# First unit of a two-block transformer kernel: norm weights sent in the tokens' rows, another order of loads, low parts moved between VectorE and GpSimd, idle products on TensorE, high products ahead of low ones

## The chip, the cores and the metric

One core of a Trainium2 chip. The metric is the device time of one execution in microseconds, the median over several runs. Below, a profile of one execution stands beside it; its times count from the first instruction.

## The reference

The reference runs two blocks over 512 tokens of width 1024 in float32. The first block puts 16 meta tokens ahead of them (528 in all), and does attention of two kinds, gates and a feed-forward part; the second block is larger. Only the very first step matters here:

```python
h = jnp.concatenate([meta, x], axis=1)
xn = rms_norm(h, norm_gains[layer, 0])          # h * rsqrt(mean(h*h) + EPS) * gain
proj = xn @ w_in[layer]
q_a, k_a, v_a, f_a, q_b, k_b, v_b, g_a, g_b = jnp.split(proj, SPLIT_POINTS, axis=-1)
```

The root of the mean square is one number per token, so the kernel multiplies it in after the product: it computes (h * gain) @ w_in first and scales the result.

## The kernel before, in words

**Units.** All weights stream through as units of 1 MB, 128 x 2048 float32, which is 16 tiles of 128x128: for each of the eight slices k of the width two tiles, c = 0 and c = 1 (a chunk is one c over all k). Two buffers each of `raw`, `whi` and `wlo` alternate between even and odd units. SP loads a unit into `raw` when `lo_done` says that the one before in that buffer has been used (L670 to L675).

**Three products for one.** To keep float32 accuracy with the faster matmul type, each weight is split in a high part (`whi`, ScalarE's cast) and a low part (`wlo` = raw - whi, GpSimd's subtraction, L692), each activation likewise in `xhi` (ScalarE, L844) and `xlo` (VectorE, L1554). TensorE then forms whi * xhi, whi * xlo and wlo * xhi (`tile_products`, L2339 to L2346, the products are on L2344), each over the tokens in two pieces of 256 and 272 columns.

**The start.** Tokens come transposed as `h`, 128 rows by 8 slices k by 528 tokens. SP issues the gains `cv`, four pairs of slices of `h`, and unit 1. ScalarE issues unit 0 in four quarters of 512 columns (a quarter holds the tiles of two k), then `fw0`, `ident` and `masks` (L831 to L836), and then goes through four rounds: cast one quarter of unit 0, make `xhi` of two k (L838 to L845). GpSimd makes the low part of each quarter behind the cast (L695 to L701), VectorE `xlo` of each k behind `xhi` (L1551 to L1556). TensorE takes k by k, with both chunks and all three products (L2432 to L2443). ScalarE then casts unit 1 whole (`hi_of(1)`, L846), loads a table, forms eight squares of `h` (L849) and some small constants; VectorE adds the squares up in seven sums (L1557 to L1561).

**What follows.** TensorE does chunk 0 of unit 1 (`chunk(1, 0, 2)`), then a product of a block of ones with the sum of the squares (L2449), which gives ScalarE and VectorE the total from which they form the roots (L862 to L865 and L1566 to L1574). Meanwhile TensorE runs the 8-column product for the forget gate (L2457) and chunk 1 of unit 1, and then needs the roots (L2463). Units 2, 3 and so on follow with the same counts of signals: `hi_first` and `lo_first` count quarters of the units that are handed on in quarters, `hi_done` and `lo_done` whole units. The lists `QUARTERED` and `HI_FIRST` (L579, L581) say which units those are, and their place in the list is their base in the count.

Every engine works through its instructions in the order of the text; waits are written by hand on named signals.

## Time and profile before

| | |
|---|---|
| median of 3 runs | 2179.92 us (2179.61 to 2180.91) |
| the profiled execution, its own time | 2180.31 us |
| its span, first to last instruction | 2178.5 us |
| instructions | 31351 |
| TensorE busy | 2148.5 us (99%), 12494 products |
| VectorE busy | 994.9 us (46%) |
| ScalarE busy | 754.2 us (35%) |
| GpSimd busy | 1007.5 us (46%) |
| mean granted clock of TensorE | 0.996 |
| data moved | 194.94 MB, mean 89 GB/s |

PE is TensorE's matmul, PEld its loading of weights, DVE VectorE, ACT ScalarE, POOL GpSimd, SP SyncE; an engine with a q behind it is its sequencer, which issues DMAs. The ends of matmuls are modelled, and consecutive ones overlap, so the distance from one start to the next says more than the duration. The granted clock is a share of full speed.

### The profile page before, as it was taken

Reading aid. Unit: us, or ns where it says so; the run is one execution under the profiler, and the core shown is the slowest. Engines: PE = TensorE matmul, PEld = TensorE weight load, DVE = VectorE, ACT = ScalarE, POOL = GpSimd, SP = SyncE. Lnnn points to the kernel's source line nnn. Section 1 sums busy time; section 2 is a strip of 40 time slices with the busy share of each in tenths; the row PEclk is TensorE's granted clock in tenths of the full one; section 3 lists DMA queues with packets and bytes.
Section 4 is the critical chain, followed back from the end, with each engine's and each line's share of the span. In section 5 each row is a group of like instructions: output and inputs, shape, how many; then the busy total and the mean of one; then the engine's idle time right before and its main releaser. Section 6 shows DMA issues by size and latency. Waiting matters only on the chain.

```text
span 2178.5 us, 31351 instructions
## 1 busy us (share of the span) xinstructions
PE 2148.5 (99%) x12494; PEld 1852.2 (85%) x12494; DVE 994.9 (46%) x1458; ACT 754.2 (35%) x1015; POOL 1007.5 (46%) x825
## 2 busy tenths in 40 slices
PE   8999999999999999999999999999999999999998
PEld 7897999999999887888888778878788888888886
DVE  5144454379888207322200819671876442222027
ACT  4133455243222215322212415551336332222134
POOL 4322223455555547555544545254331555555444
PEclk9999999999999999999999999999999999999999
DMA  4321111212222223322222221114220222222222
GB/s 164 102 69 68 59 48 70 97 59 97 96 85 88 106 96 107 125 96 96 97 97 96 91 107 42 59 59 151 81 78 21 97 97 97 96 96 97 96 100 93
DMA packets 31838, 194.94 MB, mean 89 GB/s; under 512 B 3968, under 2 KB 4480, under 8 KB 9984
## 3 DMA queue, kind: packets, MB, share of 16 engines
q1 hardware_dynamic: 26352, 182.66, 23.5%
q10 hardware_dynamic: 5392, 10.95, 1.6%
q8 instruction: 68, 1.11, 0.2%
q14 instruction: 26, 0.21, 0.0%
HBM read 189.24 MB, written 4.23 MB: 89 GB/s over the span
## 4 chain that ended last, share of the span: by engine, by line
PE 84%; issue 7%; DVE 4%; POOL 3%; ACT 1%; DMA 0%; SPq 0%; DVEq 0%; POOLq 0%; ACTq 0%
PE ps L2344 74%; POOL wlo L692 3%; PE ps L2939 2%; DVE sqa L1500 1%; PE ps L3152 1%; PE ps L3136 1%; PE ps L3072 1%; PE ps L3019 1%; DVE x2lo L1488 1%; PE ps L2623 1%; PE ps L2646 0%; PE ps L3117 0%; PE ps L2682 0%; PE ps L3162 0%; DMA h<-h 0%
## 5 line engine op out<-in xcount | busy, mean ns | idle before, releaser
L692 POOL TENSOR_TENSOR wlo<-raw,whi 128x512 fp32r<-128x512 f32 (+2 forms) x820 | 1006.1, 1259 | 1145.3 <-ACT whi L758 1041.4
L758 ACT CAST whi<-raw 128x2048 fp32r<-128x2048 f32 x162 | 309.6, 1911 | 815.1 <-PE ps L2344 757.2
L2344 PE MATMUL ps<-x2hi,whi 128*128 128x512 f32 x1136 | 449.1, 395 | 1.2 <-DVE x2lo L1488 1.1
L2344 PE MATMUL ps<-x2hi,wlo 128*128 128x512 f32 x1136 | 442.8, 390 | 0.0
L2344 PE MATMUL ps<-x2lo,whi 128*128 128x512 f32 x1136 | 442.5, 390 | 0.0
L2344 PE MATMUL ps<-xhi,whi 128*128 128x256 f32 (+2 forms) x1336 | 273.0, 286 | 11.9 <-DVE xlo L1554 9.5
L2344 PE MATMUL ps<-xlo,whi 128*128 128x256 f32 (+2 forms) x1336 | 270.6, 284 | 0.0
L2344 PE MATMUL ps<-xhi,wlo 128*128 128x256 f32 (+2 forms) x1336 | 270.4, 284 | 0.0
L2344 PEld LDWEIGHTS ps<-x2hi,whi 128*128 128x128 f32 x1136 | 213.4, 188 | 49.9 <-issue 5.6
L2344 PEld LDWEIGHTS ps<-x2lo,whi 128*128 128x128 f32 x1136 | 213.5, 188 | 44.6 <-issue 1.7
L2344 PEld LDWEIGHTS ps<-x2hi,wlo 128*128 128x128 f32 x1136 | 213.3, 188 | 44.7
L2344 PEld LDWEIGHTS ps<-xhi,whi 128*128 128x128 f32 x1336 | 208.2, 191 | 13.1 <-POOL wlo L692 12.2
L2344 PEld LDWEIGHTS ps<-xhi,wlo 128*128 128x128 f32 x1336 | 208.3, 191 | 0.0
L2344 PEld LDWEIGHTS ps<-xlo,whi 128*128 128x128 f32 x1336 | 208.3, 191 | 0.0
L2344 PE MATMUL ps<-hlo,whi 128*128 (+1 forms) x528 | 205.6, 389 | 0.0
L2344 PE MATMUL ps<-hhi,whi 128*128 (+1 forms) x528 | 205.6, 389 | 0.0
L2344 PE MATMUL ps<-hhi,wlo 128*128 (+1 forms) x528 | 205.6, 389 | 0.0
L2344 PEld LDWEIGHTS ps<-hhi,whi 128*128 128x128 f32 x528 | 99.2, 188 | 20.6
L2344 PEld LDWEIGHTS ps<-hlo,whi 128*128 128x128 f32 x528 | 99.2, 188 | 20.6
L2344 PEld LDWEIGHTS ps<-hhi,wlo 128*128 128x128 f32 x528 | 99.2, 188 | 20.3
L1512 DVE TENSOR_TENSOR cvl<-ps,fold 128x1024 f32<-128x1024 f32 x22 | 26.9, 1224 | 189.3 <-PE ps L2344 189.3
L1985 DVE SCALAR_TENSOR_TENSOR h<-ps,h 128x512 f32<-128x512 f32 x16 | 10.9, 682 | 209.7 <-PE ps L2344 209.7
(467 smaller groups left out, 2763.0 us busy)
## 6 DMA issues: line engine op xcount, KB each, us to landing
raw<-wstream SPq DMA_DIRECT2D x170, 1024.0 KB, 4.8
h<-h SPq DMA_DIRECT2D x4, 528.0 KB, 8.4
ncb<-c_rows ACTq DMA_DIRECT2D x8, 256.0 KB, 3.5
ple_rows<-ple_out ACTq DMA_DIRECT2D x4, 512.0 KB, 4.3
bias<-bias_rows ACTq DMA_DIRECT2D x8, 256.0 KB, 4.8
ple<-ple_rows ACTq DMA_DIRECT2D x4, 512.0 KB, 5.7
out_dram<-outb SPq DMA_DIRECT2D x8, 256.0 KB, 2.9
raw<-wstream ACTq DMA_DIRECT2D x4, 256.0 KB, 7.1
```

The source lines that it names most:

```text
L692: return nc.gpsimd.tensor_tensor(wlo[b][:, cols], raw[b][:, cols], whi[b][:, cols].bitcast(F32), ALU.subtract)
L758: nc.scalar.copy(whi[b][:], raw[b][:]).then_inc(sig("hi_done"), 1)
L1488: vec.scalar_tensor_tensor(out=xl[:, k, 0:T], in0=view(k), scalar=cv[:, gain + k:gain + k + 1], in1=xh[:, k, 0:T].bitcast(F32), op0=ALU.mu ...
L1500: vec.tensor_tensor(squared[:, 0, :], squared[:, 0, :], squared[:, k, :], ALU.add).then_inc(sig("sq_added"), 1)
L1512: return vec.tensor_tensor(dst, pair(src), scale, ALU.mult)
L2344: ins = mm(dst, w[slot][:, cols], xx(tok), start=first and p_ == 0, stop=last and p_ == 2, skip_group_check=True)
L2623: mm(zs[x][:, col + b * P:col + (b + 1) * P], qkb[rows_of(x), 4 + c, b * P:(b + 1) * P], qkb[rows_of(x), c, i * P:(i + 1) * P], start=(q = ...
L2939: ins = mm(gv_bank(half, j), xx[:, k if first else k + 4, tok], ww[u % 2][:, cols], start=(first and k == 0 and p_ == 0), stop=(not first ...
L3019: ins = mm(bank(5 + e)[:, t_ * P:(t_ + 1) * P], gvt[:, s_, (2 * hd + e) * P:(2 * hd + e + 1) * P], rhs, start=(x_ == 0), stop=(x_ == len(p ...
L3072: ins = mm(dst, left, right, start=True, stop=True)
L3136: mm(dst, dq[:, hd, j * P:(j + 1) * P], ckvf[:, 0:w], start=True, stop=False)
L3152: ins = mm(bank(6 + m % 2)[:, 0:P], ckvt[:, b, :], dpt[m % 2][:, b * P:(b + 1) * P], start=(b == 0), stop=(b == j))
```

## The change

1. The gains of the first norm are put in front of the tokens in the same rows: the tensor `hg` is 8 + 8 x 528 columns wide, `h` is a view of it, and `xhi` and `xlo` of the first unit take their scale from `hg`.
2. SP loads `hg` in three pieces: the gains with k = 0; k = 1 and 2; k = 3 to 7. Unit 1 follows, then `fw0`, `ident` and `masks`, which share one signal. ScalarE's queue issues quarter 0 of unit 0, its other three quarters as one DMA, and `cv`.
3. ScalarE's table load stands ahead of its first wait. Unit 1 is cast in quarters and joins the lists of units handed on in quarters.
4. VectorE makes the low parts of unit 0, one quarter ahead of each second `xlo`. GpSimd waits for these to be done and makes those of unit 1, quarter by quarter.
5. VectorE first fills a block of 128x256 with zeros (`idle`). TensorE forms ten float32 products of that block with itself into bank 7, which nobody reads, then waits for the first cast and forms one more.
6. In unit 0 TensorE forms the four high products (whi * xhi, two chunks by two pieces of tokens) of k ahead of the eight others of k - 1. In unit 1 it waits for the low parts by quarters.

```diff
@@ -160,7 +160,8 @@
     tokens = np.concatenate([v["meta_tokens"], v["x"][0]])
-    h0 = np.ascontiguousarray(tokens.T.reshape(KC, P, T1).transpose(1, 0, 2))
+    h0 = tokens.T.reshape(KC, P, T1).transpose(1, 0, 2).reshape(P, KC * T1)
+    h0 = np.concatenate([columns(v["norm_gains"][0][0]), h0], axis=1)
     units += std_units(np.concatenate([v["w_o_fox"][0], v["w_o_sb"][0]]), run_of(0, 8))
@@ -221,7 +222,8 @@
         wlo = [at(f"wlo{b}", [P, UT * P], F32R) for b in range(2)]
-        h = at("h", [P, KC, T1])
+        hg = at("hg", [P, KC + KC * T1])
+        h = hg[:, KC:].rearrange("p (k t) -> p k t", t=T1)
         x_at = place["at"]
@@ -244,6 +246,7 @@
         madds = masks_r[:, P:2 * P]
+        idle = at("idle", [P, HALF], offset=arena)
         ntri_r = at("ntri_r", [P, P], F32R, offset=temp + 14720)
@@ -576,9 +579,9 @@
         PIECE = {u: P for u in (U_UP, U_UP + 1, U_PLEP, U_F1I, U_F1I + 1, U_GR + 2, U_GR + 3, U_MG1, U_DSAO + 1)}
-        QUARTERED = [0, U_UP + 1, U_UP + 2, U_PLEP, U_F1I, U_F1I + 1, U_F1I + 2, U_PLEG + 3]
+        QUARTERED = [0, 1, U_UP + 1, U_UP + 2, U_PLEP, U_F1I, U_F1I + 1, U_F1I + 2, U_PLEG + 3]
         PIECE[U_F1I + 2] = PIECE[U_UP + 2] = BANK
-        HI_FIRST = [0, U_UP + 1, U_UP + 2, U_F1I + 1]
+        HI_FIRST = [0, 1, U_UP + 1, U_UP + 2, U_F1I + 1]
         PIECE[U_PLEG + 3] = P
@@ -663,10 +666,13 @@
         def _(sp):
-            sp.dma_start(cv[:], cvec).then_inc(sig("gains_in"), 16)
-            for q in range(4):
-                sp.dma_start(h[:, 2 * q:2 * q + 2, :], h0[:, 2 * q:2 * q + 2, :]).then_inc(sig(f"h_in{q}"), 16)
+            sp.dma_start(hg[:, 0:KC + T1], h0[:, 0:KC + T1]).then_inc(sig("h_in"), 16)
+            sp.dma_start(hg[:, KC + T1:KC + 3 * T1], h0[:, KC + T1:KC + 3 * T1]).then_inc(sig("part_in2"), 16)
+            sp.dma_start(hg[:, KC + 3 * T1:], h0[:, KC + 3 * T1:]).then_inc(sig("part_in3"), 16)
             sp.dma_start(raw[1][:], wstream[1]).then_inc(sig("raw_ready1"), 16)
+            sp.dma_start(fw0[:], fw).then_inc(sig("consts_in"), 16)
+            sp.dma_start(ident[:], ident_c).then_inc(sig("consts_in"), 16)
+            sp.dma_start(masks[:], masks_c).then_inc(sig("consts_in"), 16)
             with sp.Fori(1, n_units // 2) as i:
@@ -692,17 +698,14 @@
+            pool.wait_ge(sig("lo_done"), 1)
             for q in range(4):
                 if q < 3:
-                    pool.wait_ge(sig("hi_first"), q + 1)
-                    low_part(0, q).then_inc(sig("lo_first"), 1)
+                    pool.wait_ge(sig("hi_first"), 3 + q + 1)
+                    low_part(1, q).then_inc(sig("lo_first"), 1)
                 else:
-                    pool.wait_ge(sig("hi_done"), 1)
-                    low_part(0, q).then_inc(sig("lo_done"), 1)
-            pool.wait_ge(sig("hi_done"), 2)
-            for q in range(3):
-                low_part(1, q)
-            low_part(1, 3).then_inc(sig("lo_done"), 1)
+                    pool.wait_ge(sig("hi_done"), 2)
+                    low_part(1, q).then_inc(sig("lo_done"), 1)
             def low_parts(u, w):
@@ -828,31 +831,31 @@
+            act.dma_start(raw[0][:, 0:BANK], wstream[0][:, 0:BANK]).then_inc(sig("part_in0"), 16)
+            act.dma_start(raw[0][:, BANK:], wstream[0][:, BANK:]).then_inc(sig("part_in1"), 16)
+            act.dma_start(cv[:], cvec).then_inc(sig("gains_in"), 16)
+            nc.scalar.preload_act_table_set("natural_log_exp_and_others")
             for q in range(4):
-                act.dma_start(raw[0][:, q * BANK:(q + 1) * BANK], wstream[0][:, q * BANK:(q + 1) * BANK]
-                              ).then_inc(sig(f"part_in{q}"), 16)
-            act.dma_start(fw0[:], fw).then_inc(sig("fw_in"), 16)
-            act.dma_start(ident[:], ident_c).then_inc(sig("ident_in"), 16)
-            act.dma_start(masks[:], masks_c).then_inc(sig("masks_in"), 16)
-            act.wait_ge(sig("gains_in"), 16)
-            for q in range(4):
-                act.wait_ge(sig(f"part_in{q}"), 16)
+                if q < 2:
+                    act.wait_ge(sig(f"part_in{q}"), 16)
                 cols = slice(q * BANK, (q + 1) * BANK)
                 nc.scalar.copy(whi[0][:, cols], raw[0][:, cols]).then_inc(sig("hi_first" if q < 3 else "hi_done"), 1)
-                act.wait_ge(sig(f"h_in{q}"), 16)
                 for k in (2 * q, 2 * q + 1):
-                    nc.scalar.activation(xhi[:, k, :], h[:, k, :], ACT.Copy, scale=cv[:, G_PRE + k:G_PRE + k + 1]
+                    if k in (0, 1, 3):
+                        act.wait_ge(sig({0: "h_in", 1: "part_in2", 3: "part_in3"}[k]), 16)
+                    nc.scalar.activation(xhi[:, k, :], h[:, k, :], ACT.Copy, scale=hg[:, k:k + 1]
                                          ).then_inc(sig("xhi_ready"), 1)
-            hi_of(1)
-            nc.scalar.preload_act_table_set("natural_log_exp_and_others")
+            act.wait_ge(sig("raw_ready1"), 16)
+            for q in range(4):
+                cols = slice(q * BANK, (q + 1) * BANK)
+                nc.scalar.copy(whi[1][:, cols], raw[1][:, cols]).then_inc(sig("hi_first" if q < 3 else "hi_done"), 1)
             for k in range(KC):
                 nc.scalar.activation(sq0[:, k, :], h[:, k, :], ACT.Square).then_inc(sig("sq_done"), 1)
-            act.wait_ge(sig("fw_in"), 16)
+            act.wait_ge(sig("consts_in"), 48)
+            act.wait_ge(sig("gains_in"), 16)
             nc.scalar.copy(fwh[:], fw0[:, 0:KC * 8]).then_inc(sig("fw_hi"), 1)
...
             nc.scalar.copy(madds_tail[:], fw0[:, KC * 8 + META:]).then_inc(sig("exact_r"), 1)
-            act.wait_ge(sig("ident_in"), 16)
-            act.wait_ge(sig("masks_in"), 16)
             nc.scalar.copy(ident_r[:], ident[:]).then_inc(sig("exact_r"), 1)
@@ -1544,14 +1547,19 @@
+            vec.memset(idle[:], 0.0).then_inc(sig("cols_ready"), 1)
             step.up(vec.memset(small[:, 0:1], 1.0))
...
             vec.memset(small[:, 2:3], EPS).then_inc(sig("cols_ready"), 1)
-            dve.wait_ge(sig("gains_in"), 16)
             for k in range(KC):
+                if k % 2 == 0:
+                    q, cols = k // 2, slice(k * HALF, k * HALF + BANK)
+                    dve.wait_ge(sig("hi_first" if q < 3 else "hi_done"), q + 1 if q < 3 else 1)
+                    vec.tensor_tensor(wlo[0][:, cols], raw[0][:, cols], whi[0][:, cols].bitcast(F32), ALU.subtract
+                                      ).then_inc(sig("lo_first" if q < 3 else "lo_done"), 1)
                 dve.wait_ge(sig("xhi_ready"), k + 1)
-                vec.scalar_tensor_tensor(out=xlo[:, k, :], in0=h[:, k, :], scalar=cv[:, G_PRE + k:G_PRE + k + 1],
+                vec.scalar_tensor_tensor(out=xlo[:, k, :], in0=h[:, k, :], scalar=hg[:, k:k + 1],
                                          in1=xhi[:, k, :].bitcast(F32), op0=ALU.mult, op1=ALU.subtract
@@ -1559,6 +1567,7 @@
                 vec.tensor_tensor(sq0[:, 0, :], sq0[:, 0, :], sq0[:, k, :], ALU.add).then_inc(sig("sq_first"), 1)
+            dve.wait_ge(sig("gains_in"), 16)
             dve.wait_ge(sig("fw_hi"), 1)
@@ -2429,21 +2438,51 @@
+            def idle_turns(n):
+
+                for _ in range(n):
+                    mm(bank(7)[:, 0:HALF], idle[:, 0:P], idle[:], start=True, stop=True)
+
+            def high_tile(k, c):
+
+                for dst, tok in wide_places(STAGE1[c]):
+                    ins = mm(dst, whi[0][:, (2 * k + c) * P:(2 * k + c + 1) * P], xhi[:, k, tok], start=k == 0,
+                             stop=False, skip_group_check=True)
+                return ins
+
+            def low_tile(k, c):
+
+                cols = slice((2 * k + c) * P, (2 * k + c + 1) * P)
+                for w, xx, last in ((whi, xlo, False), (wlo, xhi, k == KC - 1)):
+                    for dst, tok in wide_places(STAGE1[c]):
+                        ins = mm(dst, w[0][:, cols], xx[:, k, tok], start=False, stop=last, skip_group_check=True)
+                return ins
+
+            pe.wait_ge(sig("cols_ready"), 1)
+            idle_turns(10)
+            pe.wait_ge(sig("hi_first"), 1)
+            idle_turns(1)
+            for k in range(KC + 1):
+                if k < KC:
+                    if k % 2 == 0:
+                        pe.wait_ge(sig("hi_first" if k < 6 else "hi_done"), k // 2 + 1 if k < 6 else 1)
+                    pe.wait_ge(sig("xhi_ready"), k + 1)
+                    for c in range(2):
+                        high_tile(k, c)
+                if k >= 1:
+                    if k % 2 == 1:
+                        low_ready(0, k // 2)
+                    pe.wait_ge(sig("x_ready"), k)
+                    for c in range(2):
+                        ins = low_tile(k - 1, c)
+                        if k == KC:
+                            ins.then_inc(sig("unit_done" if c else "half"), 1)
             for k in range(KC):
                 if k % 2 == 0:
-                    if k < 6:
-                        pe.wait_ge(sig("lo_first"), k // 2 + 1)
-                    else:
-                        pe.wait_ge(sig("lo_done"), 1)
-                pe.wait_ge(sig("x_ready"), k + 1)
-                ins = chunk_tile(0, 0, k, STAGE1[0])
-                if k == KC - 1:
-                    ins.then_inc(sig("half"), 1)
-                ins = chunk_tile(0, 1, k, STAGE1[1])
-            ins.then_inc(sig("unit_done"), 1)
-            pe.wait_ge(sig("lo_done"), 2)
-            chunk(1, 0, 2)
-            pe.wait_ge(sig("cols_ready"), 1)
+                    low_ready(1, k // 2)
+                ins = chunk_tile(1, 0, k, STAGE1[2])
+            ins.then_inc(sig("half"), 1)
+            pe.wait_ge(sig("cols_ready"), 2)
             pe.wait_ge(sig("sq_first"), 7)
...
```

## Rows read from the trace of the kernel before

**Rows 1.** Windows view of the start: per engine busy us (instructions), granted clock, DMA share, GB/s.

```profile
0.00:9.48 9.48, 0.00 (x0) 0.03 (x1) 1.44 (x6) 3.79 (x6) 1.68 (x6) 1.00 0.78 263
9.48:14.87 5.39, 5.38 (x24) 5.39 (x25) 5.39 (x4) 4.88 (x8) 4.10 (x3) 1.00 1.00 400
14.87:29.51 14.64, 14.64 (x121) 14.62 (x120) 9.64 (x13) 9.14 (x17) 6.04 (x4) 1.00 0.42 149
```

**Rows 2.** Waits view, 0 to 60 us: total us, times, longest us.

```profile
PE ps L2344 <- DVE xlo L1554: 9.5, 1, 9.5
...
ACT L841 <- DMA raw<-wstream: 5.5, 1, 5.5
...
ACT xhi L844 <- DMA h<-h: 0.2, 1, 0.2
```

**Rows 3.** Timeline of TensorE: start, us from start to end of the group.

```profile
9.48 0.78 PE L2344 MATMUL ps<-xhi,whi 128*128 128x256 f32 x2 [9.48 <-DVE xlo L1554]
...
14.87 0.40 PE L2344 MATMUL ps<-xhi,whi 128*128 128x256 f32 x2
...
29.64 1.05 PE L2449 MATMUL ps<-sq,per 128*128 128x256 f32 x4
...
42.24 1.05 PE L2463 MATMUL ps<-per,rt 1*128 1x1 f32 x8
...
95.19 0.51 PE L2344 MATMUL ps<-xhi,whi 128*128 128x256 f32 x2 [1.15 <-POOL wlo L692]
```

**Rows 4.** Timeline of ScalarE, same columns.

```profile
5.51 1.28 ACT L841 ACT_TABLE_LOAD   x1 [5.51 <-DMA raw<-wstream]
6.81 0.62 ACT L841 CAST whi<-raw 128x512 fp32r<-128x512 f32 x1
...
11.32 1.36 ACT L844 ACTIVATE xhi<-h,cv 128x528 fp32r<-128x528 f32 x2
12.59 0.60 ACT L841 CAST whi<-raw 128x512 fp32r<-128x512 f32 x1
...
15.53 1.92 ACT L758 CAST whi<-raw 128x2048 fp32r<-128x2048 f32 x1 [1.08 <-DMA raw<-wstream]
...
18.76 4.39 ACT L849 ACTIVATE sq<-h 128x528 f32<-128x528 f32 x8
```

**Rows 5.** DMA view: KB, us to landing; middle row, tile view: issue ns, first and last start.

```profile
raw<-wstream ACTq DMA_DIRECT2D x1, 256.0 KB, 4.7
L668 SPq DMA_DIRECT2D h<-h x4: 426/552/817, 1.2 to 2.9; - x4
...
h<-h SPq DMA_DIRECT2D x1, 528.0 KB, 9.9
```

**Rows 6.** Windows view, first 14 us, for the bytes that the queues moved.

```profile
2.00:5.00 3.00, 0.00 (x0) 0.00 (x0) 0.00 (x0) 0.00 (x0) 0.00 (x0) 1.00 0.87 216
5.00:12.00 7.00, 2.52 (x11) 2.55 (x12) 3.81 (x4) 6.22 (x10) 3.24 (x3) 1.00 1.04 414
```

**Rows 7.** Timeline of VectorE, single instructions, and of GpSimd (last row).

```profile
9.26 1.86 DVE L1554 SCALAR_TENSOR_TENSOR xlo<-h,cv,xhi 128x528 fp32r<-128x528 f32 x1
...
11.04 0.76 DVE L1554 SCALAR_TENSOR_TENSOR xlo<-h,cv,xhi 128x528 fp32r<-128x528 f32 x1
...
19.97 7.41 DVE L1561 TENSOR_TENSOR sq<-sq 128x528 f32<-128x528 f32 x7 [2.72 <-ACT sq L849]
...
17.53 6.04 POOL L692 TENSOR_TENSOR wlo<-raw,whi 128x512 fp32r<-128x512 f32 x4 [2.88 <-ACT whi L758]
```

**Rows 8.** Windows view around the one stage at half clock.

```profile
444.89:448.30 3.41, 3.41 (x32) 3.41 (x31) 1.43 (x2) 1.94 (x4) 1.47 (x3) 1.00 0.22 38
448.30:451.70 3.40, 1.73 (x9) 1.67 (x9) 0.51 (x2) 0.72 (x2) 2.89 (x6) 0.50 0.65 272
...
455.10:458.55 3.45, 3.45 (x18) 3.45 (x17) 3.45 (x5) 1.25 (x2) 3.45 (x5) 0.50 0.00 0
```

**Rows 9.** Timeline of TensorE before that fall of the clock.

```profile
446.16 1.17 PE L2719 MATMUL ps<-per,sq_sum 128*128 128x1 f32 x10
```

## The prediction

> **What bounds the kernel now.** I read the windows of the start first: TensorE does nothing until 9.48 us, then 24 products of the first unit in 5.39 us, then 120 more in 14.64 us without a gap [rows 1]. So there are three things to see: an empty stretch, a slow stretch and a dense one. The waits view says what ends the empty one: TensorE's only wait of the first 60 us is 9.5 us for xlo from VectorE (GpSimd's first wlo is ready at the same moment), and ScalarE's first cast had waited 5.5 us for the first quarter of unit 0 to land [rows 2]. ScalarE then spends 1.28 us on a table load that begins only when the data has landed, and its first cast begins at 6.81 [rows 4]. The timeline of TensorE shows the slow stretch: a pair of products (264 columns each on average) takes 0.22 us apiece before 14.8 us and 0.122 apiece after it (5.39 / 24 = 0.225, 14.64 / 120 = 0.122) [rows 1, 3]. Those are the two levels of its clock, 1.2 and 2.4 GHz; the granted clock is written as 1.00 for this stretch, so the product times must be read, not that column. Before the rise TensorE had been busy for 5.3 us.
>
> From 9.48 on TensorE has no gap before 95.19, where it waits 1.15 us for GpSimd's low parts [rows 3]. Those hang on ScalarE's copies, which wait for TensorE to release the buffer, so that wait moves along with TensorE. I therefore take one landmark: the product with the column of ones over the sum of squares (line 2449), whose weights TensorE takes at 29.51, the end of the third window [rows 1]. Up to it lie 96 products of unit 0 and 48 of unit 1, 144 in all. What the landmark gains, the whole program gains, if nothing later is late.
>
> A change of 0.2% is 4.4 us here, and that is about what a measurement of this kernel can tell from no change.
>
> **The change, step by step.**
>
> *Loads.* Before, 131 KB of gains, four token pairs of 528 KB and four weight quarters of 256 KB shared the queues; the last token pair, issued at 2.9, took 9.9 us and landed at 12.8 [rows 5]. ScalarE needed that. After, xhi of k = 0 needs a 268 KB piece, k = 1 the next 528 KB, and all of k = 3 to 7 the last 1320 KB in one piece. The bytes ahead of that last landing are the same 3.3 MB. By the windows the queues moved 3 x 0.216 = 0.65 MB from 2 to 5 us and 7 x 0.414 = 2.90 MB from 5 to 12 [rows 6], 3.55 MB in sum, so 3.3 MB stand at 11.4. The first quarter (256 KB beside 131 KB of gains) was through at about 3.8 to 4.2 by the same sum and landed at 0.75 + 4.7 = 5.45 [rows 5], a lag of 1.2. The first packets are now larger, worth some 0.3 us. So the last piece lands at 11.4 + 1.2 - 0.3 = 12.3, say 12.4, with 11.5 and 13.4 as the ends (no lag and gain, or the lag twice). By the same rule the first pieces land at about 5.5, and the second token piece and the other three weight quarters (1.9 MB in sum) at about 8.9. Three constants (ident, masks, fw) move from ScalarE's queue to SP's, behind unit 1's weights. Those landed at 15.5 before [rows 4], and are now needed from 16.7; the constants are needed from 23: a cover of 1 us and one of some 6 us. If the constants' cover were gone, ScalarE's casts at L851 to L858 would stop in front of its copy of qkf.
>
> *ScalarE.* It issues three DMAs in place of seven, and the table load (1.28 us) now lies in the wait for data. Its first cast moves from 6.81 to about 5.5: 1.3 us off the path [rows 4]. Its prices: two xhi in 12.59 - 11.32 = 1.27 us, so 0.64 each; a quarter cast 0.55 [rows 4]. Then xhi 0 is done at 6.8; xhi 1 waits for 8.9 and is done at 9.6; the second cast, xhi 2: 10.9; xhi 3 waits for 12.4 and is done at 13.1; the rest follows without a wait. From the start of xhi 3 the queue holds five xhi, two quarter casts and, new at this place in quarters, four casts of unit 1: 5 x 0.64 + 6 x 0.55 = 6.5, so the squares begin at 18.9, against 18.76 before [rows 4]. The copy of unit 1 as a whole took 1.92; in quarters it takes 2.2, and 0.3 us of ScalarE is the whole price of that edit.
>
> *Low parts.* VectorE now subtracts unit 0's four quarters. Its operation of this kind on 128x528 takes 0.75 us with GpSimd at rest, and up to 1.86 beside it [rows 7]. GpSimd now rests until VectorE is done with unit 0, so per pair of k VectorE has 3 x 0.75 = 2.3 us of work. TensorE needs 24 x 0.122 = 2.9 us per pair: VectorE keeps up and is no wait. GpSimd starts on unit 1 at about 17.3 and needs 6.04 for four quarters at most [rows 7], that is 1.5 per quarter; TensorE comes to unit 1 at 21.5 and takes 12 x 0.122 = 1.5 per quarter, so two quarters are ready before it asks. The reload of raw[0], which SP holds until lo_done 1, moves from 14.8 to about 16.4; its data is wanted after 30, so nothing.
>
> *Idle products.* VectorE's fill of 128x256 comes first, some 0.3 us, so TensorE starts at about 1.1. The nearest row for a product of plain f32 is the sum of squares, 1.05 us for 528 columns with its tail [rows 3], hence at most 0.5 for 256 at 2.4 GHz and 1.0 at 1.2 GHz. If the clock rises after 5.3 us of work as it did before, five products at 1.0 and five at 0.5 end at 8.6 at the latest, and the eleventh at 9.1; with no tail they end near 8.3. The second k has its xhi only at 9.6, so ten idle products cost nothing that is not hidden, or 0.1 us at the upper end. What they buy is the slow stretch: 24 products at 0.225 - 0.122, 2.5 us [rows 1].
>
> *High products first.* They let TensorE work on k while VectorE makes xlo of k - 1. The order of 144 products changes and their number doesn't. With xhi 3 at 13.1 as the last wait, 28 products of unit 0 are behind TensorE and 68 before it: 13.1 + 0.1 + 68 x 0.122 = 21.5 for unit 0, and + 48 x 0.122 = 27.35 for the landmark.
>
> *The squares.* The landmark also waits for VectorE's seven sums. They ended at 27.38, 8.6 us after ScalarE's first square at 18.76 [rows 4, 7], two of the seven stretched by GpSimd. With squares from 18.9 and GpSimd again beside about two of them, they end at 27.5. So both chains meet within 0.2 us, and I take the later: **landmark 27.5 instead of 29.5, 2.0 us off**. Behind it, TensorE needs the roots of the norm at 42.24 [rows 3], and everything in between hangs on the landmark and moves with it.
>
> For the price of a product, the Trainium skill ("TensorE: Matmul & The Clock Gate", Back-to-back issue gap) gives columns / 2.4 GHz plus 2.5 ns, 112.5 ns for 264 columns; this trace disagrees, with 122 ns over 120 products. By that figure the dense part would end 1.1 us sooner and the squares alone would set the landmark, at the same 27.5.
>
> **The sum** is against the profiled execution: span 2178.5 - 2.0 = 2176.5, its own time 2180.3 - 2.0 = 2178.3. The median of the runs is 0.4 below that one, so 2177.9.
>
> **Rivals.**
> 1. *The transfers are early and TensorE is the only bound.* For it: the larger packets, and 414 GB/s already from 5 us on [rows 6]. TensorE would run from about 8.3 without a gap, 144 x 0.122 = 17.6, landmark 25.9, 3.6 us off: 2176.3. Against it: the last piece holds five k at once and lands with the same bytes before it. Chance 0.14.
> 2. *The sum of squares takes the place of the wait.* VectorE beside GpSimd takes up to 1.86 for 0.75 [rows 7]. GpSimd's four quarters of unit 1 now lie nearer to the seven sums; if four instead of two are stretched by 0.9, or if the last piece lands at 13.4, the landmark is at 28.5 to 29.3, about 28.9: 2179.3. Chance 0.15.
> 3. *The clock falls again, and the change is slower.* In this kernel it fell at 448.3, after a stretch in which TensorE was busy all the time but from 446.16 on with products of one column, and stayed at 0.50 until 458.55, 10.25 us [rows 8, 9]. After the change TensorE stands still for about a microsecond before k = 1 and again before k = 3 (together some 1.2 to 2 of 5 us). If the clock falls there, products cost 0.22. Staying down for 5.3 us, as at the start, costs 2.4 and just cancels the gain, which is the point from which it decides; staying down for 10.25 us costs 10.25 x (1 - 0.122 / 0.225) = 4.7 against the 2.0 gained: landmark 32.2, time 2182.6. Against it: 1.15 us without work before 95.19 brought no fall: the first pair behind it takes 0.51, not the 0.78 of the first pair at half clock [rows 3]. Chance 0.05. The same page's section on oscillation says that idle gaps between bursts send TensorE back to half clock; the 1.15 us gap here shows none, and the stretch at 448 does.
> 4. *The idle products don't raise the clock.* They are plain f32 over zeros. At 1.0 each they end at 12.1, and 24 real ones still run at 0.22: 12.1 + 5.3 + 120 x 0.122 = 32.0 at the upper price, 30.5 at the lower (0.86 each); about 31.2: 2181.6. Against it: no row sets plain f32 apart, though none shows it alone at the rise. Chance 0.04.
>
> **The numbers.** The forecast case has 0.59, with its own range of 2177.0 to 2178.8 (landing 11.5 to 13.4, partly covered by the squares). The rest, 0.03, is what I don't see. From 2176.2 to 2180.0 the range holds the forecast, rivals 1 and 2, and 0.4 us of spread to either side, as the runs shown have. None of the cases leaves the band of 4.4 us except a longer fall of the clock or a wait downstream: faster 0.04, same 0.93, slower 0.03.
>
> **What would show it.** Right: table load near 2.5 us and first cast near 5.5; idle products from 1.1, half of them about twice as long as the others; real products at 0.12 from the first; a gap of TensorE before k = 3, ended by xhi 3, whose cause is the DMA of hg; VectorE's low parts at 0.7; line 2449's successor at about 27.5 with either the last sum of squares or TensorE itself just in time; everything after 30 us shifted by the same 2 us. Wrong: real products at 0.22 after 9 us (rivals 3, 4); TensorE's idle time before the squares (rival 2); no wait at k = 3 (rival 1); or a shift that is not carried to the end, with a new wait on GpSimd's low parts.

## The result, and the profile after

The changed kernel takes 2215.14 us (median of 4 runs, 2213.08 to 2216.64) against 2180.41 for the kernel before (2179.61 to 2182.51): a ratio of 1.0157, 95% interval 1.0145 to 1.0169. It is **34.7 us slower**, where 2177.9 had been forecast with 2180.0 as the upper end. Its profiled execution has a span of 2214.8 us.

The change is made within the first 30 us, so I read that stage first, by TensorE's timeline (start, length of the group, and in brackets the idle time before it and what ended it):

```profile
1.20 7.65 PE L2444 MATMUL ps<-idle 128*128 128x256 f32 x22 [1.20 <-DVE per L1554]
8.49 0.83 PE L2449 MATMUL ps<-xhi,whi 128*128 128x256 f32 x4
10.44 0.75 PE L2449 MATMUL ps<-xhi,whi 128*128 128x256 f32 x4 [1.11 <-ACT xhi L846]
11.03 0.40 PE L2458 MATMUL ps<-xlo,whi 128*128 128x256 f32 x2
11.27 0.40 PE L2458 MATMUL ps<-xhi,wlo 128*128 128x256 f32 x2
...
14.38 0.76 PE L2449 MATMUL ps<-xhi,whi 128*128 128x256 f32 x4 [0.38 <-ACT xhi L846]
...
28.85 1.13 PE L2488 MATMUL ps<-sq,per 128*128 128x256 f32 x4 [0.27 <-DVE sq L1569]
```

The landmark of the prediction, the product over the sum of squares (now L2488), starts at 28.85; before it started at 29.64 [rows 3]. **The start is 0.8 us faster, not slower.** The idle products run from 1.20 to 8.85, all real products come at 0.12 us apiece (0.24 for a pair), and there are gaps ahead of k = 1 (1.11 us), k = 2 (0.17) and k = 3 (0.38). ScalarE's timeline shows why it is 0.8 and not 2.0:

```profile
2.16 1.28 ACT L837 ACT_TABLE_LOAD   x1 [2.16 <-issue]
6.91 0.62 ACT L842 CAST whi<-raw 128x512 fp32r<-128x512 f32 x1 [3.47 <-DMA raw<-wstream]
...
9.65 0.73 ACT L846 ACTIVATE xhi<-hg 128x528 fp32r<-128x528 f32 x1 [1.48 <-DMA hg<-h]
10.92 0.62 ACT L842 CAST whi<-raw 128x512 fp32r<-128x512 f32 x1 [0.53 <-DMA raw<-wstream]
...
13.59 0.73 ACT L846 ACTIVATE xhi<-hg 128x528 fp32r<-128x528 f32 x1 [1.42 <-DMA hg<-h]
...
17.79 2.17 ACT L851 CAST whi<-raw 128x512 fp32r<-128x512 f32 x4
19.86 4.38 ACT L853 ACTIVATE sq<-hg 128x528 f32<-128x528 f32 x8
```

The table load has moved to 2.16 as forecast, but the first quarter of weights lands only at 6.9, so that the first cast is no earlier than before (6.91 against 6.81 [rows 4]); the pieces of the tokens end waits at 9.65 and 13.59, and the squares begin at 19.86, 1.1 us later than before. VectorE's sums follow them and TensorE waits for the last one:

```profile
7.56 0.69 DVE L1559 TENSOR_TENSOR wlo<-raw,whi 128x512 fp32r<-128x512 f32 x1 [6.39 <-ACT whi L842]
8.20 0.77 DVE L1562 SCALAR_TENSOR_TENSOR xlo<-hg,xhi 128x528 fp32r<-128x528 f32 x1
...
21.06 7.64 DVE L1569 TENSOR_TENSOR sq<-sq 128x528 f32<-128x528 f32 x7 [2.01 <-ACT sq L853]
```

So nothing that the change does in its own stage costs 35 us. The chain that ended last, here in order of time (start, length, what, number), shows where they are. First the kernel before, then the changed one:

```profile
868.31 326.46 PE ps L2344 x1440
...
1782.64 326.46 PE ps L2344 x1440
```

```profile
870.37 361.20 PE ps L2353 x1548
...
1808.22 361.19 PE ps L2353 x1548
```

A dense stretch of 512-column products took 326.46 / 1440 = 0.2267 us each, and now 361.20 / 1548 = 0.2333. The same stretch starts 2.1 us later at 868 and 25.6 us later at 1783, and the program ends 36.3 us later: nearly all of the loss comes with the 512-column products, from 800 us on. The windows view says the same by a count (us, then busy time and instructions of PE, PEld, DVE, ACT, POOL, then granted clock, DMA share, GB/s), again before and after:

```profile
900.00:1200.00 300.00, 300.00 (x1325) 248.54 (x1324) 54.49 (x40) 74.81 (x51) 150.65 (x111) 1.00 0.27 98
```

```profile
900.00:1200.00 300.00, 300.00 (x1288) 240.98 (x1287) 51.91 (x36) 69.68 (x45) 146.63 (x108) 1.00 0.26 94
```

In 300 us without a gap TensorE gets through 1288 products instead of 1325, at the same granted clock of 1.00 and with nearly the same load on the DMA queues. 300 / 1325 is 0.2264, 300 / 1288 is 0.2329, 6.5 ns more for each. By the groups there are 3 x (1136 + 528 + 192) products of 512 columns on that line (streams x2, hh and hl, and three smaller ones, `xr`, `gy` and `my`), 384 on two others and 48 more, 6000 in all; 6000 x 6.5 ns = 39 us. That is more than the 34.7 lost and the 0.8 gained at the start, 35.5 together: part of it falls into waits, and shorter products give some back. The chain shows the latter in a stretch of pairs of 256 and 258 columns, first before, then after:

```profile
356.65 89.67 PE ps L2344 x744
```

```profile
357.19 88.66 PE ps L2353 x744
```

These 744 products take 1.0 us less. The account that comes out to the microsecond is that of a kernel with only the addresses changed, below (b_pad32). The 36.3 between the two spans hold one more fall of the clock, shown further below.

What differs there? The instructions are the same. But `hg` has eight columns more than `h`, which is 32 bytes in each row of the on-chip memory, and everything that is allocated behind it stands 32 bytes further: `xhi`, `xlo`, `x2hi`, `x2lo`, and the arena with `hhi`, `hlo` and the streams of the second block's other products. The weight buffers stand in front of it and have not moved.

### The profile page after: what moved, and what is told of

The parts are those of the page before. It is cut to its first block, busy times and chain, and to the rows that moved or that the text cites. A ratio compares the mean times of both kernels' runs of the same rounds, so it can differ in the third digit from the quotient of the medians.

```text
span 2214.8 us, 31399 instructions
## 1 busy us (share of the span) xinstructions
PE 2189.4 (99%) x12516; PEld 1851.0 (84%) x12516; DVE 993.0 (45%) x1463; ACT 753.1 (34%) x1017; POOL 1000.9 (45%) x821
## 3 DMA queue, kind: packets, MB, share of 16 engines
q8 instruction: 68, 1.11, 0.2%
## 4 chain that ended last, share of the span: by engine, by line
PE 83%; issue 8%; POOL 5%; DVE 2%; ACT 1%; DMA 1%; POOLq 0%; DVEq 0%; SPq 0%; ACTq 0%
PE ps L2353 73%; POOL wlo L698 5%; PE ps L2978 2%; PE ps L3191 1%; PE ps L3175 1%; PE ps L3111 1%; PE ps L3058 1%; DMA hg<-h 1%; PE ps L2662 0%; PE ps L2685 0%; PE ps L3156 0%; PE ps L2721 0%; PE ps L3201 0%; DVE sqa L1503 0%; DVE hg L1547 0%
## 5 line engine op out<-in xcount | busy, mean ns | idle before, releaser
L2353 PE MATMUL ps<-x2hi,whi 128*128 128x512 f32 x1136 | 456.0, 401 | 0.7 <-DVE x2lo L1491 0.6
L2353 PE MATMUL ps<-x2lo,whi 128*128 128x512 f32 x1136 | 449.7, 396 | 0.0
L2353 PE MATMUL ps<-x2hi,wlo 128*128 128x512 f32 x1136 | 449.6, 396 | 0.0
L2353 PE MATMUL ps<-xhi,whi 128*128 128x256 f32 (+2 forms) x1304 | 263.5, 284 | 5.4 <-POOL wlo L698 3.9
L2353 PE MATMUL ps<-xhi,wlo 128*128 128x256 f32 (+2 forms) x1304 | 261.2, 282 | 0.0
L2353 PE MATMUL ps<-xlo,whi 128*128 128x256 f32 (+2 forms) x1304 | 261.2, 282 | 0.0
L2353 PEld LDWEIGHTS ps<-xhi,whi 128*128 128x128 f32 x1304 | 201.3, 188 | 6.7 <-POOL wlo L698 2.6
L2353 PEld LDWEIGHTS ps<-xhi,wlo 128*128 128x128 f32 x1304 | 201.3, 188 | 0.0
L2353 PEld LDWEIGHTS ps<-xlo,whi 128*128 128x128 f32 x1304 | 201.3, 188 | 0.0
L1994 DVE SCALAR_TENSOR_TENSOR hg<-ps,hg 128x512 f32<-128x512 f32 x16 | 10.9, 681 | 216.3 <-PE ps L2353 216.3
```

Of the source, the lines that this page charges most:

```text
L1994: vec.scalar_tensor_tensor(out=hview(m), in0=bank(m), scalar=0.5, in1=hview(m), op0=ALU.mult, op1=ALU.add).then_inc(sig("down_evac"), 1)
L2353: ins = mm(dst, w[slot][:, cols], xx(tok), start=first and p_ == 0, stop=last and p_ == 2, skip_group_check=True)
```

## The experiments

**Is it the 32 bytes?** Four kernels with only addresses changed.

```diff
+        place["at"] += 32          # a_pad32: in the kernel after, behind hg
         x_at = place["at"]

+        place["at"] += 32          # b_pad32: in the kernel before, behind h (b_pad64: 64)
         x_at = place["at"]

+        place["at"] += 32          # b_arena32: in the kernel before, behind xlo
         arena = place["at"]
```

b_pad32. 

> The kernel before with 32 bytes left free behind h and nothing else. Theory A: 512-column products at 233.3 ns, time 2180 + 33 = 2213. Rival B: 2180, 226.7 ns.

Measured: 2215.14 us, ratio 1.0158 (1.0141 to 1.0175). Its windows view from 900 to 1200:

```profile
900.00:1200.00 300.00, 300.00 (x1287) 241.02 (x1286) 51.88 (x36) 69.61 (x45) 146.70 (x109) 1.00 0.26 94
```

This is the kernel before, with its own start, and it is as slow as the changed one. The 32 bytes are the cause, and none of the five other things that the change does. Added up from start to start over this trace and that of the kernel before, the products of 512 columns take 36.1 us more, those of 256, 258 and 272 columns 2.6 less and all others 1.3 less: 32.2 us, which is the difference of the spans (2210.7 and 2178.5).

b_pad64. 

> The kernel before with 64 bytes left free behind h. Theory A (a question of multiples of 64 bytes): 2180, no change. Rival C (any shift of the operands against the weights or against each other costs): slower by up to 33 us.

Measured: 2196.69, ratio 1.0065 (1.0048 to 1.0082), 1313 products in the 300 us, 0.2285 each. So a multiple of 64 is not free: theory A, in the form that it had, falls.

a_pad32. 

> The kernel after, with 32 more bytes left free behind hg, so that xhi, xlo and all behind them stand 64 bytes further than before instead of 32. Theory A (the address of what TensorE streams, 32 bytes off a multiple of 64, costs about 6.6 ns per product of 512 columns, 5000 of them): the 512-column products go back from 233.3 to 226.7 ns from start to start, and the time is 2214 - 33 = 2180 or a little under, 2179.5 with the 0.8 us that the start gained. Rival B (something else that the change does at the start, such as the clock's phase or the idle products, slows every product): unchanged, 2214.

Measured: 2193.72, ratio 1.0059 (1.0042 to 1.0076), again 1313 products. Two thirds of the loss are back, not all of it; the rival B falls, since the start is as in the changed kernel.

b_arena32. 

> The kernel before with 32 bytes left free behind xlo, so that xhi, xlo, x2hi and x2lo stay where they were and only the arena (hhi, hlo) and what lies behind it moves by 32 bytes. Theory A, for the streamed operand alone: products with hhi and hlo at 233.3 ns, 3 x 528 x 6.6 ns = 10.5 us, those with x2hi and x2lo at 226.7; time about 2190.5. Rival D (it is the constants, the scratch or the output places at the end of the memory that count): the whole 33 us, with x2hi slow too, or none.

Measured: 2195.25, ratio 1.0064 (1.0047 to 1.0081), 14 us by the ratio where 10.5 had been forecast. The forecast left out 576 products whose streams (`xr_hi`, `gyh`, `myh` and their low parts) lie in the arena too: in this trace they also start 233 ns apart, and 576 x 6.5 ns is 3.7 us. The tile view (instructions, then duration min/median/max in ns) gives x2lo and hhi apart:

```profile
L2345 PE MATMUL ps<-x2lo,whi x279: 389/389/389, 900.1 to 1089.1; 128*128 128x512 f32 x140
```

```profile
L2345 PE MATMUL ps<-hhi,whi x176: 393/396/399, 1089.6 to 1212.1; 128*128 x128, 128*128 128x512 f32 x48
```

Products whose streamed operand has moved are 4 to 10 ns longer, those whose operand has not are at the 389 to 390 of before. Rival D falls.

**Against what?** If it isn't the address against a multiple of 64, it may be the address against something else in the memory. In the kernel before `whi`, `wlo`, `xhi`, `xlo` and the arena all start 128 bytes past a multiple of 256 (by the sizes in the code, `whi` at 32896, `wlo` at 49280, `xhi` at 82560, the arena at 119424), so "aligned" and "alike" could not be told apart there.

```diff
-        place = {"at": 16512}
+        place = {"at": 16544}      # b_all32: in the kernel before, everything

+        place["at"] += 96          # b_pad96: in the kernel before, behind h
+        place["at"] += 96          # a_pad96: in the kernel after, behind hg: 128 in all
```

b_all32. 

> The kernel before with everything in the on-chip memory moved up by 32 bytes, the weights raw, whi and wlo included. Theory A (absolute address of the streamed operand against multiples of 128 bytes): 512-column products at 233.4 ns, time about 2215, as with 32 bytes behind h. Rival E (what counts is where the streamed operand stands against the weights): 226.7 ns and 2181. If the weights' own address costs too, more than 2215.

Measured: 2179.8, ratio 0.9995 (0.9985 to 1.0005).

```profile
900.00:1200.00 300.00, 300.00 (x1325) 248.43 (x1324) 55.06 (x41) 75.33 (x52) 151.22 (x111) 1.00 0.27 97
```

1325 products, as before. **Shifted together, the operands lose nothing; it is the distance between them that costs.** Theory A is dead, rival E stands.

b_pad96. 

> The kernel before with 96 bytes left free behind h. So far an offset of 0 gave 226.7 ns, 32 gave 233.4, 64 gave 229.7. Theory A with multiples of 64 as the finer grain: 233 or a little less, 2210 to 2216. If the cost only falls with the distance from the multiple of 128 ahead: 228 ns, 2187.

Measured: 2216.84, ratio 1.0161 (1.0144 to 1.0178), 1288 products: just above what theory A gave (up to 2216) and far from 2187, so the cost doesn't fall steadily towards 128.

a_pad96. 

> The kernel after with 96 more bytes behind hg, so that xhi and all behind it stand exactly 128 bytes further than in the kernel before. Theory A: 512-column products at 226.7 ns, the 33 us are gone, and what is left is what the start gains, 0.8 us: 2180 less 1. Rival F (there is another cost downstream of the start that the alignment only covers up): above 2183.

Measured: 2217.41, ratio 1.0165 (1.0148 to 1.0182), 1293 products, 0.2320 each. I had expected 2180: a distance of 128 bytes costs nearly as much as one of 32.

The next step was the size at which the distance is free again.

```diff
+        place["at"] += 224         # a_pad224: in the kernel after, 256 in all
+        place["at"] += 480         # a_pad480: in the kernel after, 512 in all
```

a_pad480. 

> The kernel after with 480 more bytes behind hg, so that xhi and all behind it stand 512 bytes further from the weights than in the kernel before (512 bytes is one weight tile's row). Theory G (what counts is the distance between what TensorE streams and the weights it loads meanwhile, modulo 512 bytes or a divisor that 32, 64, 96 and 128 aren't multiples of): 512-column products back at 226.7 ns, time 2181 - 0.8 = 2180. If the distance counts with a larger period or the change has a second cost downstream: above 2190.

Measured: 2182.69, ratio 0.9998 (0.9989 to 1.0008), 1325 products.

a_pad224. 

> The same with 224 bytes, 256 further than before. Theory G with a period of 512: between, 228 to 234 ns and 2185 to 2217. With a period of 256: 226.7 ns and 2180.

Measured: 2180.97, ratio 0.9999 (0.9989 to 1.0008).

1325 products. Of the distances tried, 0, 256 and 512 are free, and 32, 64, 96 and 128 are not. In sum, for the distance of the streams from the weights against that of the kernel before:

| further by (bytes) | kernels | products in 300 us | us each |
|---|---|---|---|
| 0 | before, b_all32 | 1325 | 0.2264 |
| 32 | after, b_pad32 | 1288, 1287 | 0.2330 |
| 64 | b_pad64, a_pad32 | 1313 | 0.2285 |
| 96 | b_pad96 | 1288 | 0.2329 |
| 128 | a_pad96, a96_pairs (below) | 1293 | 0.2320 |
| 256 | a_pad224 | 1325 | 0.2264 |
| 512 | a_pad480 | 1325 | 0.2264 |

This fits a period of 256 bytes; distances between 128 and 256 were not tried. Both kinds of kernel agree, the one before and the one after.

**Between which operands?** Each tile gives three products in a row: xhi on whi, xlo on whi, xhi on wlo.

```diff
+        place["at"] += 32          # b_wlo32: in the kernel before, between whi and wlo
         wlo = [at(f"wlo{b}", [P, UT * P], F32R) for b in range(2)]
         h = at("h", [P, KC, T1])
+        place["at"] += 480         # so that xhi stands 512 further from whi, 480 from wlo
         x_at = place["at"]
```

b_wlo32. 

> The kernel before with 32 bytes left free between whi and wlo and 480 behind wlo: the streamed tiles stand 512 bytes further from whi, but 480 from wlo. Theory G, as a conflict between a load of weights and the stream beside it: only the product beside which wlo is loaded (the second of three, xlo or x2lo with whi) is longer, the other two stay at 226 to 227 ns; about a third of the 33 us, 2192. If the weights' place doesn't count but the absolute place of the stream does (512 bytes off): all three as before, 2181.

Measured: 2218.39, ratio 1.0166 (1.0151 to 1.0182), the full loss and not a third of it. The timeline:

```profile
999.81 0.40 PE L2346 MATMUL ps<-x2lo,whi 128*128 128x512 f32 x1
1000.05 0.39 PE L2346 MATMUL ps<-x2hi,wlo 128*128 128x512 f32 x1
1000.27 0.40 PE L2346 MATMUL ps<-x2hi,whi 128*128 128x512 f32 x1
1000.51 0.40 PE L2346 MATMUL ps<-x2lo,whi 128*128 128x512 f32 x1
1000.75 0.39 PE L2346 MATMUL ps<-x2hi,wlo 128*128 128x512 f32 x1
```

From start to start: 0.24, 0.22, 0.24, 0.24. At this rounding two of three are longer. Averaged over the 250 rounds of three from 905 to 1080 us, the distance to the next start is 239 ns behind x2lo on whi, the product beside which wlo is loaded, 233 behind x2hi on whi and 228 behind x2hi on wlo, where the kernel before has 226 to 227 for each. So the one that was expected is the longest, but it is not alone, and three products take 0.70 instead of 0.68.

b_xlo32 moved xlo and x2lo alone:

```diff
         xhi = at("xhi", [P, KC, XROW], F32R)[:, :, 0:T1]
+        place["at"] += 32
         xlo = at("xlo", [P, KC, XROW], F32R)[:, :, 0:T1]
-        x_spare = x_at + 8 * KC * SEQ
+        x_spare = x_at + 8 * KC * SEQ + 32
+        place["at"] += 224
...
-        x2lo = at("x2lo", [P, KC, SEQ], F32R, offset=x_at + 4 * KC * SEQ)
+        x2lo = at("x2lo", [P, KC, SEQ], F32R, offset=x_at + 4 * KC * SEQ + 32)
```

> The kernel before with xlo and x2lo alone 32 bytes further (xhi, x2hi, whi and wlo where they were; the arena 256 bytes further, which by the run with 256 bytes costs nothing). Theory G2 (what counts is that all that TensorE reads one after the other, stream and weights, stand alike modulo 256 bytes, and the cost is some 20 ns per three products whichever of them is off): 5 to 20 ns more per three products with x2hi and x2lo, nothing on those with hhi and hlo; 1136 x 20 = up to 22.7 us, so 2187 to 2204. Theory G3 (only the stream and the weights loaded beside it count): only the second product of three, which streams x2lo, is longer, and the time is about 2186 to 2195. No cost: then only the weights count against xhi.

Measured: 2202.42, ratio 1.0085 (1.0065 to 1.0105).

```profile
999.84 0.40 PE L2347 MATMUL ps<-x2lo,whi 128*128 128x512 f32 x1
1000.07 0.39 PE L2347 MATMUL ps<-x2hi,wlo 128*128 128x512 f32 x1
1000.30 0.40 PE L2347 MATMUL ps<-x2hi,whi 128*128 128x512 f32 x1
1000.54 0.40 PE L2347 MATMUL ps<-x2lo,whi 128*128 128x512 f32 x1
```

```profile
L2347 PE MATMUL ps<-hhi,whi x176: 389/389/395, 1093.4 to 1212.4; 128*128 x128, 128*128 128x512 f32 x48
```

Again 0.70 for three, this time on the products with x2hi and x2lo only; those with hhi are at 389. So in both cases in which one operand of the three products is 32 bytes off the other ones, the three together cost 20 ns more (700 ns instead of 680), and so does the case in which both streams are off. That supports theory G2: what TensorE reads in turn has to stand alike. G3, by which only a stream and the load beside it count, predicted a single longer product; here all three are longer (232, 236 and 232 ns), and it does not fit. How the 20 ns come about is open, and so is why 64 bytes cost 7 ns for three, 128 bytes 17 and 96 bytes 20: no row shows the memory itself.

**What the parts of the change are worth at the start**, once the memory is put right. The first of these kernels takes back the order of loads: tokens in four pairs of k, the gains in front of the first pair, and weights in quarters; the rest of the change stays.

```diff
-            sp.dma_start(hg[:, 0:KC + T1], h0[:, 0:KC + T1]).then_inc(sig("h_in"), 16)
...
+            for q in range(4):
+                cols = slice(2 * q * T1 + KC if q else 0, KC + (2 * q + 2) * T1)
+                sp.dma_start(hg[:, cols], h0[:, cols]).then_inc(sig(f"h_in{q}"), 16)
...
-            act.dma_start(raw[0][:, 0:BANK], wstream[0][:, 0:BANK]).then_inc(sig("part_in0"), 16)
-            act.dma_start(raw[0][:, BANK:], wstream[0][:, BANK:]).then_inc(sig("part_in1"), 16)
+            for q in range(4):
+                act.dma_start(raw[0][:, q * BANK:(q + 1) * BANK], wstream[0][:, q * BANK:(q + 1) * BANK]
+                              ).then_inc(sig(f"part_in{q}"), 16)
```

With 96 bytes of gap, a96_pairs. 

> As the one with 96 bytes, but loads as in the kernel before: tokens in four pairs of k (the gains in front of the first), unit 0 in four quarters, gains table last. Everything else of the change stays. If the start gained only 0.8 instead of 2.0 us because the second and third pieces of the tokens land late (9.6 and 13.6), this brings ScalarE's squares forward to about 17.5 to 18 and the product of line 2449 from 28.8 to about 26.3, another 2 us. If the loads are as late in any order, it stays at 28.8.

Measured: 2213.32, ratio 1.0150 (1.0133 to 1.0167), slow for its distance of 128 bytes; the landmark is at 26.76, near the 26.3 expected. With 480 bytes, a480_pairs. 

> 480 bytes and the loads in pairs and quarters as in the kernel before, the rest of the change as it is. Theory G: 226.7 ns per product, and the product of line 2449 at 26.8, as with 96 bytes, against 29.5 in the kernel before: 2181 - 2.8 = 2178. A second cost downstream: above 2181.

Measured: **2177.79, ratio 0.9983 (0.9974 to 0.9992): faster than both kernels**, by 0.17% than the one before.

```profile
1.19 6.95 PE L2445 MATMUL ps<-idle 128*128 128x256 f32 x22 [1.19 <-DVE per L1555]
8.14 1.30 PE L2450 MATMUL ps<-xhi,whi 128*128 128x256 f32 x8
...
26.69 1.13 PE L2489 MATMUL ps<-sq,per 128*128 128x256 f32 x4 [0.27 <-DVE sq L1570]
```

```profile
6.74 0.62 ACT L843 CAST whi<-raw 128x512 fp32r<-128x512 f32 x1 [1.48 <-DMA raw<-wstream]
...
13.96 1.37 ACT L847 ACTIVATE xhi<-hg 128x528 fp32r<-128x528 f32 x2
15.62 2.18 ACT L852 CAST whi<-raw 128x512 fp32r<-128x512 f32 x4 [0.29 <-DMA raw<-wstream]
17.71 4.38 ACT L854 ACTIVATE sq<-hg 128x528 f32<-128x528 f32 x8
```

```profile
865.63 326.45 PE ps L2354 x1440
...
1779.95 326.46 PE ps L2354 x1440
```

The landmark comes 2.95 us earlier than before (26.69 against 29.64), and the dense stretches start 2.68 and 2.69 earlier than in the kernel before: what the start gains is carried through. ScalarE begins the casts of unit 1 at 15.62 instead of 17.79, the squares start at 17.71 instead of 19.86, and that is the whole difference to the order of loads of the change (landmark 28.89 with it, in a_pad480, and 2.2 us less here).

From this kernel one part was taken away at a time: the eleven idle products (p_noidle), VectorE's and GpSimd's new split (p_gplow), high products first (p_plain).

```diff
-            idle_turns(10)                                   # p_noidle
             pe.wait_ge(sig("hi_first"), 1)
-            idle_turns(1)
...
-            pool.wait_ge(sig("lo_done"), 1)                  # p_gplow: and VectorE's low parts out
+            for q in range(4):
+                if q < 3:
+                    pool.wait_ge(sig("hi_first"), q + 1)
+                    low_part(0, q).then_inc(sig("lo_first"), 1)
+                else:
+                    pool.wait_ge(sig("hi_done"), 1)
+                    low_part(0, q).then_inc(sig("lo_done"), 1)
...
+                low_ready(0, k // 2)                         # p_plain, at each even k
+                pe.wait_ge(sig("x_ready"), k + 1)
+                ins = chunk_tile(0, 0, k, STAGE1[0])
+                ins = chunk_tile(0, 1, k, STAGE1[1])
```

p_noidle. 

> The kernel with 480 bytes and loads in pairs, without the eleven idle products. If the idle products raise the clock: the first some 24 real products take 0.22 us instead of 0.12, TensorE falls behind, and the product of line 2449 comes at about 8.3 + 5.3 + 120 x 0.12 = 28.0 instead of 26.8, time 1.2 us more, 2179. If the clock rises by itself or the squares hide the loss: the same 26.8.

Measured: 2180.53, ratio 0.9992 (0.9982 to 1.0002).

```profile
8.09 2.10 PE L2450 MATMUL ps<-xhi,whi 128*128 128x256 f32 x8 [8.09 <-ACT xhi L847]
...
10.86 0.55 PE L2459 MATMUL ps<-xlo,whi 128*128 128x256 f32 x2
11.25 0.41 PE L2459 MATMUL ps<-xhi,wlo 128*128 128x256 f32 x2
...
27.11 1.05 PE L2487 MATMUL ps<-sq,per 128*128 128x256 f32 x4
```

Without them the first 14 products take 0.22 us each, until 11.25, and the rest 0.12, here after 3.2 us of work; 24 slow ones had been expected. The landmark comes at 27.11, 0.4 us later, not the 1.2 expected. Nothing holds TensorE up there: the sums of squares end at 26.54, and its own chain comes 0.4 us too late for them.

p_gplow. 

> The same kernel with GpSimd making the low parts of unit 0 and then of unit 1 and VectorE only xlo, as before. VectorE's xlo would be stretched again to up to 1.8 us beside GpSimd, its last xlo ending about 1.5 us later than with the split; TensorE stays behind xlo by up to 1 us, and GpSimd works longer beside the squares' sums. Line 2449 at 27.5 to 28.5 instead of 26.8. If the split is worth nothing: 26.8.

Measured: 2179.4, ratio 0.9989 (0.9979 to 0.9999).

```profile
26.84 1.13 PE L2490 MATMUL ps<-sq,per 128*128 128x256 f32 x4 [0.52 <-DVE sq L1571]
```

p_plain. 

> The same kernel with the products of unit 0 in the order of the kernel before (three products of a tile together, each k waiting for its xlo). TensorE's first real product starts about 1 us later and k by k waits for xlo, but the squares' sums end at 26.7 in any case, so line 2449 at 26.8 to 27.8. If high products first are worth their place: at least 27.3.

Measured: 2179.67, ratio 0.9988 (0.9978 to 0.9998).

```profile
26.63 1.13 PE L2483 MATMUL ps<-sq,per 128*128 128x256 f32 x4
```

The landmark is at 26.84 and 26.63, against 26.69 with everything. Taken away one at a time the three parts are worth 0.4, 0.15 and nothing there. In p_gplow and p_plain, as with everything, VectorE's sums of squares end 0.14 to 0.15 us ahead of it and set it (in p_plain TensorE shows no wait: its own chain is there at the same moment). No run takes away more than one part, and their worth together is not the sum of these: without high products first the first product starts at 8.96 instead of 8.14, and a chain as slow as that of p_noidle from there on would end at about 27.11 + 8.96 - 8.09 = 28.0, an estimate, 1.3 us later than with both. The intervals of the times overlap with that of a480_pairs, so the order by time among these four is not settled; one profile of each is what the landmarks rest on.

## Why the prediction was wrong

**The step that failed** is one that was never written down as a step: that a product outside the changed stage keeps its duration, and so that "what the landmark gains, the whole program gains". "The order of 144 products changes and their number doesn't", and for all the others nothing. Of edit 1 (gains in the tokens' rows) I priced the bytes and the landing time and not the eight columns in the on-chip memory. The diff shows `h` being replaced by a wider `hg` ahead of `x_at = place["at"]`, and `at` in the kernel lays buffers out by a running address; that was enough to see that every later operand moves, though not what it would cost. It cost 6.5 ns on a dense product of 512 columns, of which there are 6000, and 36 us in b_pad32. The 0.03 left for "what I don't see" was far too little for a change that moves the addresses of nearly everything.

The rest, by the steps of the prediction:

- *Loads.* 1.2 us off. The last piece landed at 1.67 + 11.90 = 13.6, not 12.4 (the range ended at 13.4); the first pieces at 6.9, not 5.5. This row of the chain is the last one's:

```profile
1.67 11.90 DMA hg<-h
```

  I took the lag behind the bytes from 131 KB of gains beside 256 KB, and the new first piece has 268 KB beside 256 KB and much larger ones right behind it. The size was off (no run shows the 0.3 us that were taken off for larger packets), and also the judgement that the order is neutral: by pairs the same bytes feed ScalarE 2.2 us sooner.
- *ScalarE.* Right in its prices: from xhi 3 at 13.59 to the squares at 19.86 it took 6.3 where 6.5 was worked out. Right that the table load goes under the wait, wrong that this brings the first cast forward: the data is what comes later.
- *Low parts.* Right: VectorE at 0.69 and 0.77 without being stretched, no wait of TensorE on them. p_gplow shows that the old split would have done nearly as well.
- *Idle products.* Right that they end at 8.9 within the shadow of the loads and that real products run at the upper level from the first; rival 4 is out. Their worth was given as 2.5 us, for 24 slow products; in p_noidle 14 are slow, which is 1.4 us of TensorE's time, and 0.4 at the landmark, since the squares set it otherwise. The prediction had both chains meeting; it should have said that a part which speeds up only TensorE's chain is worth no more than their distance.
- *The squares.* Right as the bound, at 28.85 rather than 27.5 by the late landing. TensorE waits 0.27 us for the last sum. This part of rival 2 came true: it had the landmark at about 28.9 if GpSimd stretched more sums or the last piece landed at 13.4, and it was the load, at 13.6. The seven sums took 7.64 against 7.41.
- *The clock.* Rival 3 did not happen in the gaps before k = 1 and k = 3 of this execution, nor in three others with the same start, whose gaps before k = 1 were 1.36, 1.54 and 1.48 us (a_pad32, a_pad96, a_pad480). It did in the fifth, a_pad224: behind a gap of 1.33 us the clock fell, and pairs of products took 0.44 instead of 0.24 from 10.86 to 14.33.

```profile
10.27 0.79 PE L2450 MATMUL ps<-xhi,whi 128*128 128x256 f32 x4 [1.33 <-ACT xhi L847]
```

```profile
11.00:14.00 3.00, 3.00 (x16) 3.00 (x15) 1.43 (x3) 1.60 (x3) 0.00 (x0) 0.50 0.99 411
```

  The landmark still came at 28.96, as the squares ended at 28.54: it cost 0.3 us. So the rival's cause was real, while its price (2.4 to 4.7 us) was far too high, for the squares hide most of it. The fall at 448, which the prediction set beside the idle gaps, is of another kind: TensorE was busy for 3.41 of the 3.41 us ahead of it [rows 8]. The profiled execution of the changed kernel has one fall more than that of before, too, at 1320, behind eight products of 16 rows:

```profile
1320.70:1327.50 6.80, 6.80 (x15) 4.36 (x14) 3.51 (x4) 1.12 (x2) 0.00 (x0) 0.50 0.02 7
```

  a_pad480 has such a one too, at 1306.7 for 3.4 us, b_pad32 at the same place has none, and nearly all runs of the kernel before lie between 2179.6 and 2185.0 in these experiments. 6.8 us at half rate cost 3.4 us at most, and the fall at 450 us is shorter here than in the kernel before (6.8 against 10.2 us), so that at most 1.7 are left between the two; this belongs to the spread between runs, and may be why the 0.7 us of a_pad480's start can't be seen in its median.
- *"What the landmark gains, the whole program gains."* Right as to waits, once the addresses are mended: in a480_pairs 2.95 at the landmark, 2.7 at 866 and at 1780.

The Trainium skill's page "TensorE: Matmul & The Clock Gate" (Step-by-step: what each phase is for) says that TensorE has two independent read ports and that loading the next weights doesn't take bandwidth from the running product. No run here shows the ports. What the runs add is that placement counts all the same: at a distance of 0, 256 or 512 bytes a product of 512 columns with its weight load takes 226 ns, and at 32, 64, 96 and 128 it is 2 to 7 ns longer. Whether that is the load and the stream in each other's way is not shown. The page "SBUF — State Buffer" (Operand start alignment) asks only for a multiple of the element's size and says that its runs timed nothing; by the letter of it all these kernels are legal, and so they are, at a price of up to 1.7% (b_wlo32).

## What to carry to other kernels

A few bytes more in one buffer move every buffer behind it, and that alone can change the time of products all over the program. After any change of an allocation compare the number of products in a dense stretch far from the edit, and keep what TensorE streams and what it loads alike modulo 256 bytes by a gap behind the odd-sized buffer. That is measured for float32r products of 512 columns; those of 256 and 258 columns were a little shorter when 32 bytes apart. Before costing an edit, list what it does to addresses as well as to instructions. And where two chains meet at one wait, a part that shortens one of them is worth only their distance: here the order of the loads counted (2.2 us), and idle products, the split and the order of products, each taken away alone, 0.4 us or less. Such single removals don't say what the parts are worth together.

## What the runs showed of the hardware that was not expected

- Products of float32r with 512 columns, whose weights are reloaded each time, take 0.2264 us when weights and both streams start alike modulo 256 bytes, and 0.2285 to 0.2330 when they are 32 to 128 bytes apart (0.2267 and up to 0.2333 from start to start in the dense stretches). A shift of all of them by 32 bytes changes nothing (1325 products in 300 us in both).
- One operand of three that is 32 bytes off costs as much as two: 20 ns for the three products, whether it is wlo, xlo or both streams.
- Products of 256 and 258 columns, taken together, don't lose by 32 bytes but gain: 744 of them take 88.66 us instead of 89.67, in b_pad32 too. In pairs of 256 and 272 columns at the start it is 0.240 us a pair against 0.244.
- The clock rose 3.2 us after TensorE's first product in p_noidle and 5.4 us after it in the kernel before. The idle products covered both, but in a_pad224 they didn't keep the clock up across the gap of 1.33 us behind them, and in a_pad480 one of 1.48 us did no harm.
